# The odd layer's norm factor taken out of the rows and multiplied in behind the products of f_in, the low-rank tiles and the gates

## What is computed

```python
def rms_norm_2(x, g):
    xf = x.astype(jnp.float32)
    y = xf * lax.rsqrt(jnp.mean(xf * xf, axis=-1, keepdims=True) + RMS_EPS)
    return (y * g.astype(jnp.float32)).astype(x.dtype)

def even_layer(...):
    ...
    return x + rms_norm_2(y, g_post)

def odd_layer(x, cos, sin, g_pre, g_post, w_in, g_q, w_uq, g_kv, w_ukv, w_fd, w_out):
    h = rms_norm_2(x, g_pre)
    p = h @ w_in
    c_q, c_kv, k_r, f_in, z_c, z_d = split_cols(p, ODD_SIZES)
    qh = (rms_norm_2(c_q, g_q) @ w_uq).reshape(B, S, H_C, QK_NOPE + QK_ROPE)
    ...
    kv = (rms_norm_2(c_kv, g_kv) @ w_ukv).reshape(B, S, H_C, QK_NOPE + V_HEAD)
    ...
    y_c = att * jax.nn.silu(z_c)
    fr = jnp.real(jnp.fft.fft2(fg, axes=(1, 3), norm="ortho"))
    y_d = (fr @ w_fd) * jax.nn.silu(z_d)
    y = jnp.concatenate([y_c, y_d], axis=-1) @ w_out
    return x + rms_norm_2(y, g_post)
```

## Time and profile before

| what | us |
|---|---|
| runs, median of 3 (lowest to highest) | 869.03 (868.64 to 869.35) |
| the profiled execution's own time | 871.23 |
| its span in the trace | 869.4 |
| mean granted clock of PE over the span | 0.993 |
| PE busy | 848.8 |
| DVE busy | 544.9 |
| ACT busy | 489.8 |

### The profile page before, as it was taken

The page is one execution under the profiler, slowest core; times in us unless marked ns, Lnnn a source line. Parts: engine busy times, 40 slices in busy tenths (PEclk is TensorE's granted clock), DMA queues, the critical chain, the costliest instruction groups (busy, mean ns, idle before and its releaser), DMA issues.

```text
span 869.4 us, 14878 instructions
## 1 busy us (share of the span) xinstructions
PE 848.8 (98%) x5900; PEld 765.9 (88%) x5900; DVE 544.9 (63%) x974; ACT 489.8 (56%) x832; POOL 18.5 (2%) x23
## 2 busy tenths in 40 slices
PE   8999999999999999999989999999999989999997
PEld 7999898888889999988768799899998879999785
DVE  5433456866866666675785854367885574558764
ACT  6653547764565545455564335576666564655554
POOL 0000000004300000000000000000000000000000
PEclk9999999999999999999989999999999999999999
DMA  9654752226435554555525425334445635435312
GB/s 346 265 214 171 277 182 98 98 98 202 172 127 186 195 175 171 188 185 203 187 103 194 160 83 195 131 113 145 147 153 191 235 111 184 177 127 205 118 49 73
DMA packets 21696, 144.19 MB, mean 166 GB/s; under 512 B 2529, under 2 KB 3169, under 8 KB 4992
## 3 DMA queue, kind: packets, MB, share of 16 engines
q1 hardware_dynamic: 20736, 140.55, 45.3%
q10 hardware_dynamic: 896, 2.73, 0.9%
HBM read 142.22 MB, written 1.05 MB: 165 GB/s over the span
## 4 chain that ended last, share of the span: by engine, by line
PE 90%; DVE 5%; ACT 3%; DMA 1%; issue 1%; DVEq 0%; ACTq 0%
PE PS L441 88%; DVE wl L1771 1%; ACT wh L1206 1%; DMA ring<-w 1%; ACT hh L1220 1%; DMA xa<-x 0%; PE PS L1120 0%; PE PS L741 0%; ACT PB L1246 0%; DVE PB L1820 0%; PE PS L743 0%; PE PS L742 0%; ACT PB L1240 0%; DVE cn L2081 0%; DVE xb L2099 0%
## 5 line engine op out<-in xcount | busy, mean ns | idle before, releaser
L1771 DVE TENSOR_TENSOR wl<-ring,wh 128x1024 fp32r<-128x1024 f32 x248 | 305.5, 1235 | 260.4 <-ACT wh L1206 252.5
L1206 ACT ACTIVATE wh<-ring 128x1024 fp32r<-128x1024 f32 x248 | 261.4, 1057 | 242.6 <-PE PS L441 225.8
L441 PE MATMUL PS<-hh,wh 128*128 128x256 f32 x1212 | 349.8, 289 | 2.8 <-DVE hl L1834 1.3
L441 PE MATMUL PS<-hl,wh 128*128 128x256 f32 x1212 | 343.1, 283 | 0.0
L441 PE MATMUL PS<-hh,wl 128*128 128x256 f32 x1212 | 343.0, 283 | 0.0
L441 PEld LDWEIGHTS PS<-hh,wh 128*128 128x128 f32 x1212 | 231.3, 191 | 9.0 <-issue 5.7
L441 PEld LDWEIGHTS PS<-hl,wh 128*128 128x128 f32 x1212 | 231.5, 191 | 1.4 <-issue 1.2
L441 PEld LDWEIGHTS PS<-hh,wl 128*128 128x128 f32 x1212 | 231.3, 191 | 0.0
L441 PE MATMUL PS<-wh,hh 128*128 128x512 f32 (+2 forms) x448 | 165.0, 368 | 3.6 <-DVE hl L1791 1.7
L441 PE MATMUL PS<-wl,hh 128*128 128x512 f32 (+2 forms) x448 | 161.4, 360 | 0.0
L441 PE MATMUL PS<-wh,hl 128*128 128x512 f32 (+2 forms) x448 | 161.3, 360 | 0.0
(11 more groups left out here) (301 smaller groups left out, 696.3 us busy)
## 6 DMA issues: line engine op xcount, KB each, us to landing
ring<-w SPq DMA_DIRECT2D x127, 1024.0 KB, 4.8
cn<-consts SPq DMA_DIRECT2D x2, 1051.0 KB, 9.4
V<-gains ACTq DMA_DIRECT2D x3, 512.0 KB, 5.9
cn<-consts SPq DMA_DIRECT2D x1, 1050.5 KB, 9.1
xa<-x SPq DMA_DIRECT2D x2, 512.0 KB, 4.6
ring<-w SPq DMA_DIRECT2D x2, 512.0 KB, 5.9
out<-xb SPq DMA_DIRECT2D x4, 256.0 KB, 2.1
BIG<-rows SPq DMA_DIRECT2D x1, 448.0 KB, 10.6
```

The source lines that it names most:

```text
L441: return nc.tensor.matmul(o, lhsT, rhs, start=start, stop=stop, skip_group_check=True)
L1206: A(wh[:, q % SPLITS, :], ring[:, i % RING, e:e + HALF], ACT.Copy).then_inc(sem("hi_ready"), 1)
L1771: TTn(wl[:, q % SPLITS, :], ring[:, PLACE[unit_of(q)] % RING, e:e + HALF], wh[:, q % SPLITS, :].bitcast(F32), ALU.subtract).then_inc(sem(" ...
```

## The change

The odd layer's rows are turned as they are (`rows_turned`): the first tile's right behind the last product of the even layer, then three warm products, then the second tile's in two parts, one for each half of x4. `hh` and `hl` hold x4 times gain, without the norm's factor. ACT's squares and roots move behind `turned_evac`, between the weight halves of f_in, and DVE's reciprocals behind them. DVE multiplies the unit matrix with the factors of each tile into `PTS`, and PE multiplies that with a matrix of 1/256, which spreads the factor of each token over all partitions, divided by 256. ACT copies it back to `PTS` times 256. f_in has its tokens on the partitions and gets its factor as the scale of ACT's copies. The low-rank tiles and the gate units have their tokens along the row: DVE multiplies them with the spread factor (`times_rstd`), out of PS. For a gate unit ACT's tanh then reads that product from SBUF, and DVE's `(tanh + 1) * z` (`z_gated`) follows one unit later. Besides, some semaphores that count different things are joined under one name (`zeroed` and `branch_sum` become `pool_step`, `eps_set` and `half_bias` become `dve_consts`), with the same waits.

```diff
-JOINT_WARM = 6
+JOINT_WARM = 3
...
+            def rows_turned(t):
+
+                for b in range(KD // 2):
+                    if b == 0 or (t and b == 2):
+                        pe.wait_ge(sem("x4_ready"), 1 if t == 0 else 2 + b // 2)
+                    for k in (2 * b, 2 * b + 1):
+                        o = (k % 2) * S + t * P
+                        m = nc.tensor.transpose(PS[:, TURNED[3][b], o:o + P], xa[:, t, k * P:(k + 1) * P], ident)
+                    if t == TT - 1:
+                        m.then_inc(sem("rows_turned"), 1)
+
+            rows_turned(0)
             for u in (o_unit(3), z_unit(3)):
                 pe.wait_ge(*read(u))
             for _ in range(JOINT_WARM):
                 mm(PS[:, G[0], 0:S], ident, c("mean", 0, S), True, True)
-
-
-            norm_transposes(3)
+            rows_turned(1)
             normed(3)
             wide_pair(half_of("f_in"), F_AT)
+            pe.wait_ge(sem("row_rstd"), 6)
+            mm(PS[:, SC[1], 0:S], c("mean", P, 2 * P), PTS[:, 0, 0:S], True, True).then_inc(sem("rstd_spread"), 1)
             wide_b(FIRST["lora"])
...
             part_root(4)
-            act.wait_ge(sem("x4_ready"), 1)
+
+
+
+            turned_evac(3, "g4", half_of("f_in"))
+            act.wait_ge(sem("x4_ready"), 3)
             row_square(5, 0, cols2(xa[:, 0, :]))
             row_root(5, 0)
-            for h in range(2):
-                act.wait_ge(sem("x4_ready"), h + 2)
-                part_square(5, h, xa[:, 1, h * 512:(h + 1) * 512])
-            part_root(5)
-
-
-            turned_evac(3, "g4", half_of("f_in"))
             for n in range(4):
                 multiplied(half_of("f_in") + n)
+                if n < 2:
+                    part_square(5, n, xa[:, 1, n * 512:(n + 1) * 512])
+                if n == 1:
+                    part_root(5)
+            act.wait_ge(sem("rstd_spread"), 1)
+            A(PTS[:, 1, 0:S], PS[:, SC[1], 0:S], ACT.Copy, scale=float(S)).then_inc(sem("rstd_rows"), 1)
             for t in range(TT):
-                A(FT[:, t, :], PS[:, F_AT + t, :], ACT.Copy).then_inc(sem("fft_copied"), 1)
+                A(FT[:, t, :], PS[:, F_AT + t, :], ACT.Copy, scale=rms[:, 2 * 5 + t:2 * 5 + t + 1])\
+                    .then_inc(sem("fft_copied"), 1)
             for i in range(3):
                 u = FIRST["lora"] + i
                 multiplied(half_at(u))
                 multiplied(half_at(u) + 1)
-                freed(A(LQ[:, 2 * i:2 * i + 2, :], cols2(bank_of(u)), ACT.Copy), u)
...
                 multiplied(half_at(u) + 1)
-                A(T1[:, i % 2, :], bank_of(u), ACT.Tanh, scale=0.5).then_inc(sem("zcd_tanh"), 1)
+                act.wait_ge(*read(u))
+                A(cols2(T1[:, i % 2, :]), z_tiles(i), ACT.Tanh, scale=0.5).then_inc(sem("zcd_tanh"), 1)
...
             post_norm(4, 1, xb, xa, "x4_ready", 2)
-            scaled(5, 0, xa)
+            halves(half_of("f_in") + 1)
+
+
+            turned_evac(3, "g4", half_of("f_in"))
             part_bias(5)
-            scaled(5, 1, xa)
-            halves(half_of("f_in") + 1)
-
-
-            turned_evac(3, "g4", half_of("f_in"))
-            for i in range(5):
+            halves(half_of("f_in") + 2 + SPLITS)
+            for t in range(TT):
+                dve.wait_ge(sem(f"row_rms[{t}]"), 6)
+                q = rms[:, 2 * 5 + t:2 * 5 + t + 1]
+                nc.vector.reciprocal(q, q).then_inc(sem("row_rstd"), 1)
+            dve.wait_ge(sem("row_rstd"), 4)
+            for t in range(TT):
+                TS(PTS[:, 0, t * P:(t + 1) * P], ident, rms[:, 2 * 5 + t:2 * 5 + t + 1], None, ALU.mult)\
+                    .then_inc(sem("row_rstd"), 1)
+            for i in range(2):
                 keep_up(FIRST["f_in"] + i)
+
+            def times_rstd(o, u):
+
+                dve.wait_ge(sem("half_used"), half_at(u) + 2)
+                freed(TTn(o, cols2(bank_of(u)), PTS[:, 1, 0:S].unsqueeze(1).broadcast_to([P, 2, S]), ALU.mult), u)
+
+            dve.wait_ge(sem("rstd_rows"), 1)
+            for i in range(3):
+                keep_up(FIRST["lora"] + i)
+                times_rstd(LQ[:, 2 * i:2 * i + 2, :], FIRST["lora"] + i)
+
+            def z_gated(i):
+
+                dve.wait_ge(sem("zcd_tanh"), i + 1)
+                own(STT(z_tiles(i), cols2(T1[:, i % 2, :]), 1.0, z_tiles(i), ALU.add, ALU.mult))
+
             for i in range(6):
 
                 u = FIRST["z_c"] + i
                 keep_up(u)
-                dve.wait_ge(sem("zcd_tanh"), i + 1)
-                o = ZC[:, 2 * i:2 * i + 2, :] if i < 4 else ZD[:, 2 * i - 8:2 * i - 6, :]
-                freed(STT(o, cols2(T1[:, i % 2, :]), 1.0, cols2(bank_of(u)), ALU.add, ALU.mult), u)
+                times_rstd(z_tiles(i), u)
+                if i:
+                    z_gated(i - 1)
                 for k in ((), (0, 1), (2, 3), (4,), (), ())[i]:
...
+            z_gated(5)
             for k in range(5):
                 low(k, LQ[:, k, :], "lora_hi", k, "lora_ready")
```

More of the change, by code:

```diff
@@ L627, in smalls_turn @@
                 m.then_inc(sem("small_done"), 1)
-            pe.wait_ge(sem("zeroed"), 2)
+            pe.wait_ge(sem("pool_step"), 2)
             for _ in range(WARM):
@@ L656, in cmp_hidden @@
             def cmp_hidden(i, half):
-                pe.wait_ge(sem("zeroed"), 3)
+                pe.wait_ge(sem("pool_step"), 3)
                 pe.wait_ge(sem("flat_ready"), i + 1)
@@ L1185, in uq_dest, with z_tiles @@
             return V[:, n % 2, (n - 10) // 2 * 512:((n - 10) // 2 + 1) * 512]
+        def z_tiles(i):
+            return ZC[:, 2 * i:2 * i + 2, :] if i < 4 else ZD[:, 2 * i - 8:2 * i - 6, :]
         def add_pe(eng, i):
@@ L1283, in flat_copies @@
                 return ins
-            act.wait_ge(sem("eps_set"), 2)
+            act.wait_ge(sem("dve_consts"), 2)
             root_table(0)
@@ L1361, in cmp_kv @@
                 ins.then_inc(sem("cmp_kv"), 1)
-            act.wait_ge(sem("half_bias"), 1)
+            act.wait_ge(sem("dve_consts"), 3)
             halves(half_of("gates") + SPLITS)
@@ L1836, in turned_evac @@
                 halves(first + SPLITS)
-            nc.vector.memset(eps_t[:, 0:1], EPS).then_inc(sem("eps_set"), 1)
-            nc.vector.memset(eps_t[:, 1:2], LN_EPS).then_inc(sem("eps_set"), 1)
+            nc.vector.memset(eps_t[:, 0:1], EPS).then_inc(sem("dve_consts"), 1)
+            nc.vector.memset(eps_t[:, 1:2], LN_EPS).then_inc(sem("dve_consts"), 1)
             row_reciprocal(0)
@@ L1849, in _ @@
                 .then_inc(sem("w_small_split"), 1)
-            TS(half_b, v("b_gates", 0, 24), 0.5, None, ALU.mult).then_inc(sem("half_bias"), 1)
+            TS(half_b, v("b_gates", 0, 24), 0.5, None, ALU.mult).then_inc(sem("dve_consts"), 1)
             keep_up(0)
@@ L1863, in _ @@
             dve.wait_ge(sem("fox_logs"), 2)
-            dve.wait_ge(sem("zeroed"), 2)
+            dve.wait_ge(sem("pool_step"), 2)
             for half in range(2):
@@ L1890, in _ @@
             dve.wait_ge(sem("consts_in"), 16 * RING)
-            dve.wait_ge(sem("zeroed"), 1)
+            dve.wait_ge(sem("pool_step"), 1)
             for g in range(2):
@@ L2301, in _ @@
             post_norm(4, 1, xb, xa, "x4_ready", 2)
-            scaled(5, 0, xa)
-            part_bias(5)
-            scaled(5, 1, xa)
             halves(half_of("f_in") + 1)
             turned_evac(3, "g4", half_of("f_in"))
-            for i in range(5):
-                keep_up(FIRST["f_in"] + i)
+            part_bias(5)
+            halves(half_of("f_in") + 2 + SPLITS)
[8 more added lines that the diff above has]
+            for i in range(2):
+                keep_up(FIRST["f_in"] + i)
+            def times_rstd(o, u):
[8 more added lines that the diff above has]
+                own(STT(z_tiles(i), cols2(T1[:, i % 2, :]), 1.0, z_tiles(i), ALU.add, ALU.mult))
             for i in range(6):
@@ L2426, in _ @@
         def _(pool):
-            nc.gpsimd.memset(T1[:, 1, 0:2 * P], 0.0).then_inc(sem("zeroed"), 1)
-            nc.gpsimd.memset(CM, 0.0).then_inc(sem("zeroed"), 1)
+            nc.gpsimd.memset(T1[:, 1, 0:2 * P], 0.0).then_inc(sem("pool_step"), 1)
+            nc.gpsimd.memset(CM, 0.0).then_inc(sem("pool_step"), 1)
             pool.wait_ge(sem("rows_turned"), KD // 2)
-            nc.gpsimd.memset(flat2[:, :, :, 30:32].rearrange("p i j c -> p (i j) c"), 0.0).then_inc(sem("zeroed"), 1)
+            nc.gpsimd.memset(flat2[:, :, :, 30:32].rearrange("p i j c -> p (i j) c"), 0.0).then_inc(sem("pool_step"), 1)
             for i in range(KD):
@@ L2435, in _ @@
                 nc.gpsimd.tensor_tensor(a[:, 0:S], a[:, 0:S], a[:, S:2 * S], ALU.add)\
-                    .then_inc(sem("branch_sum"), 1)
-                pool.wait_ge(sem("branch_sum"), i + 1)
+                    .then_inc(sem("pool_step"), 1)
+                pool.wait_ge(sem("pool_step"), 3 + i + 1)
                 nc.gpsimd.tensor_tensor(Y[:, 8 + i, :], a[:, 0:S], a[:, 2 * S:3 * S], ALU.add)\
```

## The result

| what | kernel before | changed kernel |
|---|---|---|
| runs side by side, median of 7 each (lowest to highest) | 869.35 (868.64 to 870.79) | 872.60 (870.70 to 872.99) |
| ratio, with its 95% interval | | 1.0024 (1.0013 to 1.0034) |
| the profiled execution's own time | 871.23 | 872.61 |
| its span | 869.4 | 870.8 |
| mean granted clock of PE over the span | 0.993 | 0.993 |

The changed kernel is slower by about 0.24%, some 2 us, and the time lies above the predicted range, 866.9 to 870.6. In two further sets of runs, beside the experiments, the ratio was 1.0010 (1.0000 to 1.0020) and 1.0016 (1.0007 to 1.0026), and the medians were 870.65 and 870.76, just above the range.

What follows compares the result with a forecast made beforehand. PE, busy for 98% of the span, was taken to bound the kernel. The terms -2.55 + 0.43 + 1.99 = -0.13 us, against a median of 869.03, gave 868.9 us; range 866.9 to 870.6.

Steps and rivals of the forecast that it cites:

- The joint: Between even and odd layer: f_in's first weight split, and so its products, start 2.55 us earlier, bounds 2.2 to 2.7.
- The spread product: Before the low-rank units: one more PE product spreads the factor and costs 0.43 us on PE's path.
- f_in's fourth weight split: In f_in: ready at 709.3, in time by 0.4 us, costed at nothing; rival of late f_in or gate weights 14%.
- The end of the gate units: After the last gate unit: tanh waits for DVE's product, so PE goes on 1.99 us later, bounds 1.6 to 2.3.
- the tail is hidden: Rival at the gates' end: the late copy does not hold PE, only -2.1 is left, 866.9 us; 13%.
- By the rows the clock holds: At the joint: three warm products end 2.3 us ahead of f_in, so PE's clock does not fall.
- clock 1.00 at both: Sign expected in the changed profile: PE's clock at 1.00 at the joint and behind the last gate unit.
- The clock falls at the joint: Rival: with three warm products instead of six, PE is at 1.2 GHz when f_in starts; 871.1 us, slower; 12%.
- the clock is under 1 in either pause: Sign of being wrong: PE's clock below 1 in the pause at the joint or at the gates' end.

Runs made afterwards that it cites:

- pair_after: The changed kernel unaltered, run again in the third set as base of the three others; median 870.76 us, ratio 1.0016 to the kernel before.
- tail_warm: The changed kernel with four useless PE products between the first and second Fourier products; median 869.67 us, ratio 1.0000 to the kernel before.
- tail_last_w0: The changed kernel with ACT's last tanh behind the Fourier copies, DVE's last gating behind the low parts, and no warm products at the joint; 869.24 us, ratio 0.9992.

## Why the prediction was wrong

- *The joint: -2.55 (2.2 to 2.7).* Right, -2.56. DVE stayed the last arm.
- *The spread product: +0.43.* Right, +0.43. f_in's fourth weight split had 1.0 us in hand and not 0.4, for ACT's half square ended sooner than I had it. No gate unit waited; DVE's product adds 0.61 us to the chain.
- *The end of the gate units: +1.99 (1.6 to 2.3).* Right as a wait, +2.04. The rival "the tail is hidden" was wrong: the copy does hold PE. That tanh reads SBUF now, left unpriced, cost 0.63 in place of 0.58 us.
- *"By the rows the clock holds".* The step that failed. It was asked of one pause only. At the joint it was right: 1.00 there. But the step before had made a new pause of "2.25 us" at the gates' end, and I took that as 2.25 us of wait and nothing more. I wrote "clock 1.00 at both" with rows for the joint alone. The clock fell there in each of three profiles, and the products behind it took 1.67 us more. -0.13 + 1.67 + 0.05 for the longer wait is 1.6 us, about the 1.3 of the later sets (means 871.10 - 869.82 and 871.28 - 870.01) and less than the 2.6 of the first (872.19 - 869.59).
- *Forecast 868.9, measured 872.60: 3.7 us.* Only some 1.7 of that is the failed step. The kernel before was itself 0.3 us up, and 5 of the 7 changed runs were at 0.993 or less, as are the two profiles of that kernel with 6.8 us at the low level ahead of the even layer. These two reach the end of the even layer's products at 696.48 and 696.56, pair_after with 3.4 us there at 694.64, 1.8 to 1.9 us sooner. That the first median lay so far out is chance.
- *"The clock falls at the joint", 871.1, 12%.* The mechanism was right, and of its price the 1.7 for the fall (it costs 1.6 to 1.7); the place was wrong, and that the measured time came near 871.1 is luck. The runs without warm products show that the clock does fall at the joint when it has none. What I held against this rival, 1.00 over a longer pause, came from a place where warm products stand. It was good for the joint, which held with three, and said nothing of a pause without any.
- *The signs for being wrong.* I named "the clock is under 1 in either pause", and that is what came.

Left open: why a pause of 2.3 us lowered the clock in all three profiles, and one of 2.07 us in the old kernel not in its profile and not in the 3 of 10 runs at 0.999. The lengths differ by 0.24 us, and what went before is the same 16 products and slightly different gate units; no run here separates the two. Nor does the end of the pause decide it: in pair_after the clock was still 1.00 when PE went on. Also open is why the lowest time of the changed kernel, 869.38, is only 0.9 us above the lowest of the kernel with useless products, 868.50, where the trace gives 1.6.

## What to carry to other kernels

An edit that makes PE wait has two prices, the wait and what the clock does behind it: go through every pause that the edit lengthens, not only the one that it was made for, and compare each with the longest one that the trace shows to hold *without* products in it. That is a warning and no safe limit, as the fall near 250 us shows. Where a wait can't be avoided, useless products in it are nearly free if they are done before it ends (four in tail_warm cost nothing, three more at the joint 0.64 us), and where it comes from one operation at the wrong place of a queue (here a tanh that nobody needs yet, ahead of copies that PE waits for), moving that is worth more: 2.3 us more than the useless products gave (869.91 - 867.61). What a fall will cost depends on whether its low stretch lies on products or on waits.

## What the hardware showed that I had not expected

In the first changed profile the clock fell 2.4 us after the last product had ended (770.15 to 772.5), in pair_after 3.2 us after it (768.28 to 771.4), 0.85 us after PE had gone on. At the joint ahead of the even layer it had been 3 us. In tail_last_w0 it came 4.9 us after the last product of the even layer (694.6 to 699.5), with turns in between. At the gates' end and at this joint the clock was low for 3.4 us. Ahead of the even layer it was low for 6.8 us in five of the 14 profiles (before and after among them), for 3.4 in eight and not at all in one. A fall of 3.4 us cost 1.6 to 1.7 us, half of its length, at the two places where it lay wholly on products, and less where PE waited or turned in part of it: some 0.75 us near 250 us, 0.2 to 0.9 ahead of the even layer.

Runs of one kernel fall into groups 1 to 2 us apart: pair_after has one at 869.44, six from 870.54 to 870.89 and four from 872.52 to 872.87. So a median of 7 or 11 runs jumps by as much, from 872.60 to 870.65 for the very same kernel, and the means and the mean clocks tell more.
